# Layer normalisation from running sums, and the first two projections behind it taken together

## The reference

```
z = x @ w_in                                  # conv branch, attention branch, gates
m = sigmoid(g_A) * conv_module(z) + sigmoid(g_B) * sparse_attention(z)
x = LN(ALPHA * x + m @ w_o)                   # which = 0
x = LN(ALPHA * x + (silu(x @ w_gate) * (x @ w_up)) @ w_down)    # which = 1

def layer_norm(x, g, b):
    mu = mean(x); var = mean((x - mu) ** 2)
    return (x - mu) * rsqrt(var + 1e-5) * g + b
```

## Time and profile before

| | |
|---|---|
| median of 3 runs | 1190.06 us |
| the profiled execution | 1188.55 us |
| its span, first to last instruction | 1186.7 us |
| mean granted TensorE clock | 0.936 of full |
| busy: PE, PEld, DVE, ACT, POOL | 1039.2, 965.6, 555.3, 495.1, 770.9 us |

### The profile page before, as it was taken

The page is one execution under the profiler, slowest core; times in us unless marked ns, Lnnn a source line. Parts: engine busy times, 40 slices in busy tenths (PEclk is TensorE's granted clock), DMA queues, the critical chain, the costliest instruction groups (busy, mean ns, idle before and its releaser), DMA issues.

```text
span 1186.7 us, 22922 instructions
## 1 busy us (share of the span) xinstructions
PE 1039.2 (88%) x7438; PEld 965.6 (81%) x7438; DVE 555.3 (47%) x1070; ACT 495.1 (42%) x902; POOL 770.9 (65%) x1077
## 2 busy tenths in 40 slices
PE   5997798977798999999889968899669799999994
PEld 5996577765787999999779947787558699999993
DVE  2997946435624232210249987543446332222003
ACT  4333345533436544433353232654334364444334
POOL 6998216622493989998559971455127569999882
PEclk9988789988898999999989987999779989999997
DMA  8646458421152664444256534674002324444441
GB/s 305 219 164 216 128 179 281 169 92 54 43 191 82 212 238 163 177 160 169 81 183 219 172 96 133 207 266 174 36 36 102 129 108 160 172 167 160 175 145 76
DMA packets 78140, 185.07 MB, mean 156 GB/s; under 512 B 9283, under 2 KB 42435, under 8 KB 77507
## 3 DMA queue, kind: packets, MB, share of 16 engines
q1 hardware_dynamic: 74130, 171.22, 41.4%
q10 hardware_dynamic: 3744, 11.40, 2.7%
q0 software_dynamic: 144, 0.96, 0.2%
HBM read 170.97 MB, written 12.57 MB: 155 GB/s over the span
## 4 chain that ended last, share of the span: by engine, by line
POOL 63%; issue 35%; POOLq 1%; DMA 1%; ACT 0%; SPq 0%
POOL w_lo L567 57%; POOL hid L590 3%; POOL res L588 2%; POOLq L561 0%; DMA table<-page_table_in 0%; DMA wch<-weights_in 0%; POOLq L585 0%; POOLq L147 0%; POOL hid L588 0%; ACT w_hi L974 0%; POOL hid L591 0%; SPq L429 0%; POOLq L573 0%; SPq L170 0%; POOLq L578 0%
## 5 line engine op out<-in xcount | busy, mean ns | idle before, releaser
L567 POOL TENSOR_TENSOR w_lo<-wch,w_hi 128x256 fp32r<-128x256 f32 x940 | 705.8, 784 | 404.6 <-ACT w_hi L974 402.9
L627 PE MATMUL proj<-x_hi,w_hi 128*128 128x288 f32 x1376 | 416.7, 303 | 39.3 <-DVE x_lo L1598 17.3
L628 PE MATMUL proj<-x_hi,w_lo 128*128 128x288 f32 x1376 | 411.4, 299 | 0.0
L629 PE MATMUL proj<-x_lo,w_hi 128*128 128x288 f32 x1376 | 410.9, 299 | 0.0
L974 ACT ACTIVATE w_hi<-wch 128x1024 fp32r<-128x1024 f32 x235 | 248.3, 1057 | 230.3 <-PE proj L629 118.3
L627 PEld LDWEIGHTS proj<-x_hi,w_hi 128*128 128x128 f32 x1376 | 263.7, 192 | 51.1 <-issue 27.2
L628 PEld LDWEIGHTS proj<-x_hi,w_lo 128*128 128x128 f32 x1376 | 264.5, 192 | 0.0
L629 PEld LDWEIGHTS proj<-x_lo,w_hi 128*128 128x128 f32 x1376 | 263.9, 192 | 0.0
L1295 DVE SCALAR_TENSOR_TENSOR hid<-u_p,sm,hid 128x256 f32<-128x256 f32 x240 | 164.6, 755 | 3.4 <-DVE sq L1324 1.0
L645 PE MATMUL proj<-hid_lo,w_hi 128*128 128x288 f32 x352 | 104.2, 296 | 0.0
L643 PE MATMUL proj<-hid_hi,w_hi 128*128 128x288 f32 x352 | 103.8, 295 | 0.0
(11 more groups left out here) (236 smaller groups left out, 1298.3 us busy)
## 6 DMA issues: line engine op xcount, KB each, us to landing
wch<-weights_in SPq DMA_DIRECT2D x235, 512.0 KB, 3.2
pg<-cmp_pages_in SPq DMA_DIRECT2D x128, 128.0 KB, 2.6
pg<-slc_pages_in SPq DMA_DIRECT2D x128, 128.0 KB, 2.1
wn<-win_in SPq DMA_DIRECT2D x4, 2048.0 KB, 8.4
win_out<-wn ACTq DMA_DIRECT2D x4, 2048.0 KB, 8.1
hid<-w_in SPq DMA_DIRECT2D x2, 1024.0 KB, 5.9
kv_out<-kv ACTq DMA_DIRECT2D x2, 864.0 KB, 5.4
res<-xT_in SPq DMA_DIRECT2D x1, 1152.0 KB, 5.1
```

The costliest lines, as they stand in the source:

```text
L567: last = nc.gpsimd.tensor_tensor(lo[:, cols], raw[:, cols], hi[:, cols].bitcast(F32), ALU.subtract)
L627: mm(ps, hi[:, kb], x_hi[:, kb], start=kb == 0, stop=False)
L628: mm(ps, lo[:, kb], x_hi[:, kb], start=False, stop=False)
L629: last = mm(ps, hi[:, kb], x_lo[:, kb], start=False, stop=kb == KD - 1)
```

## The change

The norms over features (both in each layer; the norm in the convolution module keeps its way) are rebuilt:

- When the first two outputs are projected (behind the second one also in the down projection), TensorE computes the sum of chunk 0's features over 1024 (`seed_mean`). VectorE subtracts 8 times that, chunk 0's own mean, from each chunk (`shift`): chunk 0 after its output is added, the others before. A shift that is the same for all features of a token changes neither variance nor the normalised value.
- While further outputs come, VectorE keeps a running sum of chunks 0 to 6 (`sums`), ScalarE squares each chunk (`features_square`), and VectorE keeps the running sum of squares (`add_square`).
- Behind the last output TensorE does four matmuls: the two sums and the last chunk and its square (`features_statistics`). Variance is mean square less squared mean. ScalarE loads the root's table with a one-element activation (`warm`) ahead of the root, and the tanh's table after the last x chunk.
- VectorE subtracts, scales and makes x_lo in a mixed order, pair by pair (end of `features_norm`).
- At the start of a layer, of w_o and of gate/up, `project_two` takes two projections together: both weight chunks are waited for, and each x chunk is multiplied with both before the next.
- ScalarE's squares stand between its `high_part`s; the chunk FIRST_GU + 2 is rounded behind the root, and the next layer's chunk 1 ahead of the last square.

```diff
@@ -672,14 +679,49 @@
                         pe.wait_ge(*conv_lo_ready(layer, 1))
                     branch_out(layer, o - O_MIX)
...
+            def conv_statistics(layer, source, ps, ready):
+                for kb in range(KC):
                     ready(kb)
-                    last = mm(ps, mean, source[:, kb], start=kb == 0, stop=kb == n - 1)
+                    last = mm(ps, k("mean_c"), source[:, kb], start=kb == 0, stop=kb == KC - 1)
                 stat_done.up(last)
+            def features_summed(layer, which, kb):
+                o = (O_WO, O_DOWN)[which] + kb
+                return out_read[o % 2](layer, o // 2 + 1)
+            def seed_mean(layer, which):
+                pe.wait_ge(*features_summed(layer, which, 0))
+                stat_done.up(mm(seed_ps, k("mean_d"), resv[:, 0], start=True, stop=True))
+            def features_statistics(layer, which):
+                pe.wait_ge(*partial_ready(layer, 2 * which + 1))
+                mm(mean_ps, k("mean_d"), sums, start=True, stop=False)
+                pe.wait_ge(*partial_ready(layer, 2 * which + 2))
+                mm(square_ps, k("mean_d"), sqv[:, 0], start=True, stop=False)
+                pe.wait_ge(*features_summed(layer, which, KD - 1))
+                stat_done.up(mm(mean_ps, k("mean_d"), resv[:, KD - 1], start=False, stop=True))
+                pe.wait_ge(*squared(layer, 2 + KD * which + KD))
+                stat_done.up(mm(square_ps, k("mean_d"), sqv[:, KD - 1], start=False, stop=True))
+            def project_two(layer, o, j, first):
+                ps = [start_out(layer, o), start_out(layer, o + 1)]
+                for i in range(2):
+                    pe.wait_ge(*lo_ready(layer, j + i + 1))
+                for kb in range(KD):
+                    pe.wait_ge(*x_lo_ready(layer, first + kb + 1))
+                    last = []
+                    for i in range(2):
+                        hi, lo = w_hi[:, (j + i) % PAIRS], w_lo[:, (j + i) % PAIRS]
+                        mm(ps[i], hi[:, kb], x_hi[:, kb], start=kb == 0, stop=False)
+                        mm(ps[i], lo[:, kb], x_hi[:, kb], start=False, stop=False)
+                        last.append(mm(ps[i], hi[:, kb], x_lo[:, kb], start=False, stop=kb == KD - 1))
+                for i in range(2):
+                    out_done.up(last[i])
             def compress(layer, i):
@@ -840,8 +882,9 @@
             with layers(pe) as layer:
                 state["out"] = 0
-                for o in range(8):
-                    project_x(layer, o, o, -KD if o == 0 else None)
+                project_two(layer, 0, 0, -KD)
+                for o in range(2, 8):
+                    project_x(layer, o, o, None)
                 pe.wait_ge(*nsa_ready(layer, 1))
                 pe.wait_ge(*uo_ready(layer, 0))
...
                 pe.wait_ge(*conv_ready(layer, 1))
                 pe.wait_ge(*conv_s_ready(layer, 1))
                 pe.wait_ge(*roped(layer, 6))
-                statistics(layer, KC, conv, k("mean_c"), lambda kb: None)
+                conv_statistics(layer, conv, conv_mean, lambda kb: None)
                 second(layer, 4)
                 fill(layer)
-                statistics(layer, KC, sqv, k("mean_c"), lambda kb: pe.wait_ge(*squared(layer, kb // 2 + 1)))
+                conv_statistics(layer, sqv, conv_var, lambda kb: pe.wait_ge(*squared(layer, kb // 2 + 1)))
                 pe.wait_ge(*centered(layer, 2))
                 for gr in range(2):
                     last = mm(ps_g[:, 24 * gr:24 * gr + 24], k("spread")[P - NEW:, gr * P:gr * P + P], gates[P - NEW:, 2], start=True, stop=True)
@@ -932,22 +975,19 @@
                 for n in range(KD):
                     branch_out(layer, KD + n)
...
+                project_two(layer, O_WO, CH_IN + CH_MIX, 0)
+                seed_mean(layer, 0)
+                for n in range(2, KD):
+                    project_x(layer, O_WO + n, CH_IN + CH_MIX + n, None)
+                features_statistics(layer, 0)
+                project_two(layer, O_GU, FIRST_GU, KD)
+                for n in range(2, 2 * KF):
+                    project_x(layer, O_GU + n, FIRST_GU + n, None)
+                for n in range(KD):
+                    down(layer, n)
+                    if n == 1:
+                        seed_mean(layer, 1)
+                features_statistics(layer, 1)
             for sig in (out_done, down_used, gates_turned, gout_turned, gates_done, turned, v_turned, bias_done, h_done, w2_done, stat_done, spread_done, gm_done, gs_done,
                         gsum_done, gt_done, gpv_done, us_done, ut_done, upv_done):
                 sig.end()
...
@@ -1031,17 +1071,34 @@
                 do(v_misc[32:64, b:b + 2], v[0:32], ACT.Copy, scale=0.5, wait=False)
                 do(v_misc[64:95, b:b + 2], v[32:63], ACT.Copy, cmp_ready, scale=0.5)
-            def norm_sd_squares(layer, which, source, n):
-
-                for part in range(n // 2):
+            def conv_squares(layer):
+                for part in range(2):
                     cols = slice(2 * part * TOK, 2 * (part + 1) * TOK)
...
+                    act.wait_ge(*centered(layer, part + 1))
+                    do(sq[:, cols], conv.rearrange("p k t -> p (k t)")[:, cols], ACT.Square, squared, wait=False)
+            def features_square(layer, which, n):
+                if n:
+                    o = (O_WO, O_DOWN)[which] + n
+                    act.wait_ge(*out_read[o % 2](layer, o // 2 + 1))
+                else:
+                    act.wait_ge(*seed_ready(layer, which + 1))
+                do(sqv[:, n], resv[:, n], ACT.Square, squared, wait=False)
+            def features_root(layer, which):
+                act.wait_ge(*stat_done(layer, 3 * which + 4))
+                do(sqv[:, 1], mean_ps, ACT.Square, mean_squared, wait=False)
+                do(warm[:], eps[:, 0:1], ACT.Sqrt, wait=False)
+                act.wait_ge(*var_ready(layer, which + 1))
+                do(rstd, rstd, ACT.Sqrt, sd_ready)
+            def conv_root(layer):
+                act.wait_ge(*stat_done(layer, 2))
+                do(rstd, conv_var, ACT.Sqrt, sd_ready, bias=eps[:, 0:1])
             def unit_act(layer, u, part):
                 t = u % HALF
...
@@ -1221,8 +1278,10 @@
                             do(x_hi[:, c], gate_a[:, c], ACT.Copy, x_hi_ready, wait=False)
                             if c % 2:
                                 high_part(layer, CH_IN + (KD + c) // 2 + PAIRS)
-                        for n in range(CH_IN + CH_MIX + PAIRS, CH_IN + CH_MIX + CH_WO + PAIRS):
-                            high_part(layer, n)
+                        for n in range(KD - 1):
+                            high_part(layer, CH_IN + CH_MIX + PAIRS + n)
+                            features_square(layer, 0, n)
+                        features_square(layer, 0, KD - 1)
                     else:
                         for i in range(KF):
                             act.wait_ge(*out_done(layer, O_GU + 2 * i + 1))
@@ -1236,23 +1295,29 @@
                             if i == 2:
                                 act.wait_ge(*x_lo_ready(layer, 2 * KD))
                                 do(res[:], res[:], ACT.Copy, ax_ready, scale=ALPHA)
...
+                        n = 0
+                        for c in range(CH_DOWN - 1):
+                            if n < KD - 1 and 8 * c + 7 >= KF * (n + 1) + 4:
+                                features_square(layer, 1, n)
+                                n += 1
+                            j = CHUNKS - CH_DOWN + PAIRS + c
+                            high_part(*((layer, j) if j < CHUNKS else (layer + 1, j - CHUNKS)))
+                        assert n == KD - 1
+                        features_square(layer, 1, KD - 1)
+                    features_root(layer, which)
+                    if which == 0:
+                        high_part(layer, FIRST_GU + PAIRS - 1)
                     gn, bn = (s("g1"), s("b1")) if which == 0 else (s("g2"), s("b2"))
                     for c in range(KD):
-                        if c % 2 == 0:
-                            act.wait_ge(*normed(layer, 3 + 4 * which + c // 2))
+                        if c < 2 or c % 2 == 0:
+                            act.wait_ge(*normed(layer, 2 + 5 * which + (c + 1 if c < 2 else 2 + c // 2)))
                         do(resv[:, c], resv[:, c], ACT.Identity, x_ready, scale=gn[:, c:c + 1], bias=bn[:, c:c + 1], wait=False)
                         if c:
                             act.wait_ge(*x_ready(layer, KD * which + c))
                             do(x_hi[:, c - 1], resv[:, c - 1], ACT.Copy, x_hi_ready, wait=False)
                     act.wait_ge(*x_ready(layer, KD * which + KD))
                     do(x_hi[:, KD - 1], resv[:, KD - 1], ACT.Copy, x_hi_ready, wait=True)
+                    do(warm[:], eps[:, 0:1], ACT.Tanh, wait=False)
                 high_part(layer + 1, 2)
                 act.sem_inc(act_order.sem, ACT_ORDER - act_order.count)
```

(66 more changed lines are left out.)

79 lines of the change are left out of this document (18 added, 61 removed).

## The result

The kernel after takes 1218.62 us (median of four, 1217.08 to 1224.61), the kernel before 1190.36 beside it: ratio 1.0247, 95% interval 1.0211 to 1.0282, 28 us slower. On two other occasions the ratio was 1.0274 (1.0252 to 1.0296) and 1.0285 (1.0258 to 1.0313), so 28 to 34 us. The forecast was 1204.5 us, 14.5 slower, with 1210 as its upper end.

What follows compares the result with a forecast made beforehand. TensorE was taken to set the pace in gate/up and the down projection. The terms summed as 2.85 + 8.6 - 5.6 + 8.0 - 2.5 - 1.9 + 5.1 = +14.5, giving 1204.5 us on the median, range 1193 to 1210.

Steps and rivals of the forecast that it cites:

- The start, +2.85: First layer's start: the pair waits for weight chunk 1, so chunk 3 is projected by 32.9, not 30.04; +2.0 to +4.4.
- w_o, +4.3 twice: At w_o the pair waits 3.6 us for chunk 43, and the seed mean adds 0.5; +3.0 to +5.0 per layer.
- The seed, +4.0 twice: Down projection: output 0's square waits for the seed and holds ScalarE's rounding; TensorE waits 3.5, plus 0.5 for the seed.
- Rival B: Down projection: ScalarE is not held by the seed; -8.0 and two standstills (-2.5), giving 1194 us; chance 12%.
- The joint, -2.8 twice: Before gate/up: TensorE restarts at 8.5, x_lo comes unevenly at 1.4 us a chunk, third projection ends earlier; -1.7 to -3.5.
- Rival A: At the joints the x chunks keep the pace of 0.86 us; 20.4 us less, giving 1184 us; chance 9%.
- Into layer 2, -2.5: Joint into layer 2: the small weights' fetch on the last x chunk moves up by 1.86; -1.0 to -3.6.
- The last store, -1.9: End of the kernel: the store issued on the last identity sets the end and comes 1.9 us earlier.
- The clock, +5.1: Four new TensorE standstills of 3.5 to 3.8 us: three followed by half clock, some 1.7 lost each; 0 to +10.
- Added work at nothing: VectorE's added sums, shifts and sums of squares per output cost nothing; GpSimd loses 0.2 each, 3.2 per w_o chunk against 3.17.
- Rival C: w_o: GpSimd fully blocked by VectorE's added operations, 3.75 a chunk against 3.17, 2.9 a layer, 1210 us; chance 6%.
- the high ends of the listed terms: Whole kernel: upper limits of all terms add to +26 us, but were held not to come together.

Runs made afterwards that it cites:

- the run with the square later: Kernel after with the square of the down projection's output 0 two weight chunks later in ScalarE's queue: 1214.02 us, ratio to before 1.0179.
- the run with VectorE's order: Kernel after with VectorE's second subtraction before the reciprocal and each scaling ahead of the x_lo it stood behind: 1210.76 us, ratio to before 1.0162.
- the combined kernel: Kernel after with pair at gate/up only, square two chunks later, VectorE's joint order changed, warm-up tile last: 1175.57 us, ratio to before 0.9880.
- the runs of before: Kernel before with unused bytes: 4 behind eps 1195.16 us, 32 there 1196.39, 4 behind the weight ring 1199.78; with page table first 1190.02.
- those of after: Kernel after with its one-element warm-up tile declared last, 1218.59 us, ratio to before 1.0202, beside the unchanged kernel after, 1.0274 and 1.0285.

## Why the prediction was wrong

The direction was right and most mechanisms too; the size was half. The step that failed is the sum. It put nothing for the one-element tile that moves the weights (4 to 10 us measured, see the last point), and it had four terms too favourable: the start (2.85; 4.0 to chunk 3 and 6.3 to w_o in the mean of the profiles, 6 to 9 when undone), w_o with its clock (2 x 5.6; 6.5 to 7.1 each), the joint (-2.8; -1.9 to -2.4 each) and the end (-1.9; -0.8, by a wrong path). Step by step:

- **The start, +2.85.** Chunk 3 ended 5.1 later in the first profile, 2.4 to 4.4 in the other two of after against the two of before: to there mechanism and size were right within the spread of the first load. Undone, it gave 6 to 9. The term was mis-sized by 3 or more, since what lies behind chunk 3 was not in it, of which 1 is the page wait and the rest is open.
- **w_o, +4.3 twice.** Measured 6.5 to 7.1. The wait is 3.87 (forecast 3.6). The pair then took 8.85 to 9.39 where the two chunks of before took 7.01; 48 matmuls at 133.6 ns and the drain are 6.6, so the fall of the clock cost 2.3 to 2.8. Chunk 44 adds 0.9, as forecast. Without the clock the step is then 4.3, as forecast (though the working there adds to 354.7, 4.0 behind the old end, and not to 354.95); the sum carried the clock separately, 1.7 a fall and three falls of four, so 1.3. With it the step stands at 5.6 against 6.5 to 7.1: it is the fall that was too small.
- **The seed, +4.0 twice.** 4.15 in the layer where the clock held, 5.7 where it fell. Right, and the run with the square later confirms it: 10.9 for both, where the terms with their clock give 10.6. Rival B is out.
- **The joint, -2.8 twice.** Measured 1.9 to 2.4 less. The restart came at 9.9, not 8.5: the last output is added 0.9 behind t instead of at once, since the running sums hold VectorE, and the two single scalings beside GpSimd took 0.92 each instead of 0.45. The uneven row was right, each end 1.3 later; behind w_down, without these two, it came within 0.3 of the forecast. Rival A, an even pace near 0.86, is out for this kernel; the run with VectorE's order, at 1.0, shows that the order kept most of it away.
- **Into layer 2, -2.5.** Measured 3.1 and 2.0.
- **The last store, -1.9.** The store came 2.0 earlier, the end 0.8. The path was wrong: already in the kernel before the last, unused weight chunk ended half a microsecond behind the store's landing, and the warm-up of tanh holds it back further.
- **The clock, +5.1.** The clock fell behind all four new standstills in the first profile, behind three of four in the second. The count was right. The 1.7 a fall is the time that the 13 matmuls need at full clock; the row's own loss is 3.22 less that, 1.5. The stall in w_down lost as much by its fall (5.65 less 4.15), w_o's pair 2.3 to 2.8.
- **Added work at nothing.** Right for w_o's chunks: in the combined kernel, with all sums, chunks 45 to 49 come every 3.17 us, though GpSimd is busy there for 26.07 of 26.54 us. Not right for the joint, which the late last add delays. Rival C, these chunks bound at 3.75, is out. Beside VectorE's operations with two SBUF inputs a quarter of GpSimd's chunk takes 0.92 us and alone 0.74 (medians of the combined kernel), VectorE's operation 0.93 for 0.46: GpSimd loses 0.2, less than the 0.46 of the operation. By the Trainium skill (SBUF — State Buffer, Who interferes with whom) the port pair of these two engines is an exclusive lock, by which the forecast had GpSimd blocked for the whole operation. The trace disagrees.
- **What no step had.** The weights' place: 4 bytes declared ahead of them slow every matmul by 1%, 4 to 8 us in the runs of before and 5 to 10 in those of after, of the 28 to 34. The line was in the diff and I read it as a name. And one more wait, for GpSimd at gate/up's nineteenth chunk in layer 1: 1.1 to 4.0 us (mean 2.6) in the thirteen profiles with the new normalisation, 0.8 to 1.6 in the six without. Its cause wasn't tried and stays open.

The forecast's terms that were there, taken at their measured size in the later profiles (3.3, 14.2, -4.2, 9.9, -2.0, -0.8), give 20 with the clock in them, and 6 stand in stretches for which the sum had no term; the two spans are 27 apart. The pace would account for up to 7 of it, spread over all stretches. The medians are 28 to 34 apart; what the profiles leave of that is not resolved. The chance of 0.85 for slower was well placed, the range was not: the high ends of the listed terms gave +26, which I held to be too much at once, and nothing stood for a cost that I had not listed.

## What to carry to other kernels

A pair of projections pays only where their input is late (gate/up, 5 us or more) and costs a weight chunk's wait wherever the weights are late (w_o 13, start 6 or more). When a result is moved earlier, write out who waits for whom in the new interleaving of two engines: the order of VectorE's instructions was worth more here (10 to 15 us) than the whole new normalisation, which alone loses 4 to 5. Read tile declarations in a diff as changes of every address behind them.

## What was unexpected of the hardware

- Matmuls of 288 columns step every 132.3 ns with w_hi at byte 138944 or 139200, in six kernels, and every 133.6 to 134.0 ns with it 32 bytes further on than the first, in nine; 4 to 8 us in 1190.
- A standstill of the same 3.32 us, at the same place, was followed by clock 0.67 over 5 us in one execution and by 1.00 in another. From the first profile of after, two windows behind w_o's standstill and one behind that in w_down:

```profile
340.00:342.00 2.00, 1.87 (x8) 1.88 (x9) 0.00 (x0) 0.00 (x0) 2.00 (x3) 0.50 0.48 131
342.00:346.00 4.00, 4.00 (x21) 4.00 (x21) 0.00 (x0) 0.00 (x0) 0.75 (x2) 0.62 0.57 197
555.00:560.00 5.00, 4.55 (x23) 4.55 (x24) 0.00 (x0) 0.00 (x0) 5.00 (x8) 0.67 0.48 146
```

- One execution of the same kernel waits 4.55 us for a page load and another not at all, so a single profile's first layer is uncertain by 6 us here.
